# A two-layer encoder trunk in float32 on one core: a tile's work put behind the preparation of the weight group that follows it

## The chip, the cores and the metric

The kernel runs on one core of a Trainium2 chip. The metric is device time in microseconds (us): the median of the runs of one kernel. All multiplications of the large matrices are done in float32r with each operand split in a high part (the value rounded to what TensorE keeps) and a low part (the rest), so that one product is three matmuls: high by high, high by low, low by high.

## What is computed

The input is 256 rows of 2048 columns. Each of the two layers mixes (layer 0: a convolution branch and a gated recurrence; layer 1: two kinds of attention), normalizes, and then runs the feed-forward stage on which this change bears:

```
x = layer_norm(ALPHA * x + mixer(x), ln_mix_g[l], ln_mix_b[l])
h = jnp.square(jax.nn.relu(x @ mlp_w1[l])) @ mlp_w2[l]
x = layer_norm(ALPHA * x + h, ln_mlp_g[l], ln_mlp_b[l])
```

`mlp_w1[l]` is 2048 by 8192 and `mlp_w2[l]` 8192 by 2048, so a layer reads 128 MB of weights there, and those weights are used once.

## The kernel before

**Tiles, units, chunks.** The 8192 hidden columns are cut into 4 blocks b of 2048. A block has four tiles of the first product, w1 (b, 0) to (b, 3), 512 hidden columns each, and four of the second, w2. Each tile is done in two halves. A half is a unit of 4 chunks; a chunk is 256 by 512 weights (512 KB), brought by one DMA of SP's queue into one of four places of `raw`. Two of the w2 tiles of a block (three tiles' worth in the last) are done plainly; tiles j = 0 and 1 (in the last block j = 0 only) are instead done by a seven-product (Strassen-like) scheme, each in four groups q = 0 to 3. A group ("seven", b, j, q) takes 2 chunks of weights and the hidden tile q, and is 7 products of 6 matmuls. `block_order` (L89) writes the order of the units out by hand, `UNITS` (L103) joins it: in a block it is w1 halves and groups of the block before, then w1 (b, 2), (b, 0, 0), w1, (b, 0, 1), both halves of w1 (b, 3), (b, 0, 2), w2 (b, 2) half 0, (b, 0, 3), w2 (b, 2) half 1, and so on.

**Who prepares what.** For each chunk ScalarE copies `raw` to `w_hi` (`split`, L686), VectorE subtracts to get `w_lo` (`split`, L1022), which also lets SP load `raw` anew: `load` (L489) waits for `lo_ready` of the chunk four before. A group needs more. On VectorE `seven_raw` (L1473) waits for both chunks to land and for the products of the previous group (`chunk_used`, as both groups use one buffer), then forms sums of quarters of the weights (L1484, L1486, L1487) and low parts (L1489, L1492). On ScalarE `seven_raw` (L901) copies the high parts (L906, L908). `seven_forms` makes high (L913) and low (L1498) parts of the four sums.

**What a finished tile of w1 asks for.** On ScalarE `hidden_square` (L877: relu from PSUM L883, square L885), `hidden_hi` (L895), and `sums_hi` (L899). On VectorE `sums_added` (L1448: four sums of quarters of the hidden tile, L1456 to L1460, behind the square), `hidden_lo` (L1462: L1034, and L1466 for odd tiles; tile 3's L1034 is in two pieces) and `sums_lo` (L1471), which signals `s_ready`.

**The order around the change.** Both engines take their instructions in the order in which their `mlp` function writes them (L915, L1501). It walks the units; at unit n it does the tile that `finished(n)` (L128) names, the one whose second half ended just before n (groups in between skipped), and prepares what `behind_unit(n)` (L115) names: the groups and the one plain unit that follow n. So during unit n on TensorE the weights behind it are made ready.

**What TensorE waits for.** `seven_products` (L2104) first waits for `s_ready` of hidden tile (b, q), then for the chunks' `lo_ready`, then twice for the forms (`t_lo`), before the 4th and before the 6th product. `out_chunk` (L2067) waits for `h_ready`, `hidden_half` (L2057) for `lo_ready`, both chunk by chunk, and a tile's first matmul for its PSUM bank (`acquire_mlp`, L2047).

Of the kernel before, what the change touches and what calls it, by code (L numbers as in the profile page):

```python
# [102 lines left out]
UNITS = [unit for b in range(FB) for unit in block_order(b)]  # L103
# [11 lines left out]
def behind_unit(n):  # L115

    last = len(UNITS) - SPLIT_BEHIND
    if n < SPLIT_AHEAD:
        return [n + 2] if n == 1 else []
    if n >= last - 1:  # L120
        return [m for m in ((last, last + 1) if n == last - 1 else (n + 2,)) if m < len(UNITS)]
    m = n + 1
    while UNITS[m][0] == "seven":
        m += 1
    return list(range(n + 1, m + 1))


def finished(n):  # L128

    while n and UNITS[n - 1][0] == "seven":  # L130
        n -= 1
    if n and UNITS[n - 1][0] == "w1" and UNITS[n - 1][3] == 1:
        return UNITS[n - 1][1:3]
    return None
# [93 lines left out]
def used_before(s):  # L228
    return BEFORE[s]
# [20 lines left out]
def trunk(nc, x, ev_w_in, ev_conv_w, ev_conv_b, ev_conv_ln_g, ev_conv_ln_b, hgrn_lb_logits, ev_gnorm_g, ev_w_out,  # L250
          od_w_in, fox_b_f, rel_bias, od_w_out, ln_mix_g, ln_mix_b, mlp_w1, mlp_w2, ln_mlp_g, ln_mlp_b, out):
    w_in, w_out = [ev_w_in[0], od_w_in[0]], [ev_w_out[0], od_w_out[0]]
    with ExitStack() as ctx:
# [110 lines left out]
        def form(buf, f, n=1):  # L364

            return buf[:, BESIDE + f * FORM:BESIDE + (f + n) * FORM].rearrange("p (f k n) -> p f k n", f=n, k=CK)
# [12 lines left out]
        seven = [p[:, :].rearrange("p (u n) -> p u n", n=S) for p in pair]  # L379
# [102 lines left out]
        def raw_wait(eng, s):  # L482

            eng.wait_ge(raw_full[s % RING], 16 * (s // RING + 1))
# [187 lines left out]
        def _(act):  # L672
            at = [0]
            n = [0]
# [226 lines left out]
            def seven_raw(layer, m):  # L901

                s = SLOT_MLP[layer] + UNIT_SLOT[m]
                raw_wait(act, s)
                act.wait_ge(chunk_used, used_before(s) + 1)
                act.activation(form(seven_hi, 0)[:, 0], raw[:, s % RING, :, 0:S], ACT.Copy).then_inc(hi_ready, 1)  # L906
                raw_wait(act, s + 1)
                act.activation(low_rows(seven_hi), raw[:, (s + 1) % RING], ACT.Copy).then_inc(hi_ready, 1)  # L908

            def seven_forms(layer, m):  # L910
                for two in range(2):
                    act.wait_ge(t_ready, 2 * seven_no(layer, UNITS[m]) - 1 + two)
                    act.activation(form(seven_hi, 3 + 2 * two, 2), form(forms, 3 + 2 * two, 2), ACT.Copy).then_inc(t_hi, 1)  # L913

            def mlp(layer):  # L915
                base = SLOT_MLP[layer]
                for n, (kind, b, i, half) in enumerate(UNITS):
                    if kind == "seven":
                        if half == NT - 1:
                            act.wait_ge(chunk_used, base + UNIT_SLOT[n + 1])  # L920
                            act.activation(u_sum[:, 0], seven[0][:, 1], ACT.Copy).then_inc(p1_copied, 1)
                        continue
                    done = finished(n)
                    if done and done != (0, 0):
                        hidden_square(layer, *done)
                        hidden_hi(layer, *done)
                    if n == SPLIT_AHEAD:
                        done = (0, 0)
                        hidden_hi(layer, 0, 0)
                    ahead = behind_unit(n)  # L930
                    for m in ahead:
                        if UNITS[m][0] == "seven":
                            seven_raw(layer, m)
                    if done and n != SPLIT_AHEAD - 1:
                        sums_hi(layer, *done)
                    for m in ahead:
                        if UNITS[m][0] == "seven":
                            seven_forms(layer, m)
                            continue
                        for c in range(HALF):  # L940
                            if n == 1 and c == 2:
                                hidden_square(layer, 0, 0)
                            split(base + UNIT_SLOT[m] + c)
                if layer == 0:
                    for c in range(RING):
                        split(base + MLP_SLOTS + c)
                at[0] = base + MLP_SLOTS + RING
# [55 lines left out]
        def _(dve):  # L1003
            at = [0]
            n = [0]
# [442 lines left out]
            def sums_added(layer, b, i):  # L1448

                if b == 0 and i == 0:  # L1450
                    dve.wait_ge(h_back, layer + 1)
                else:
                    dve.wait_ge(h_row, hidden_no(layer, b, i) + 1)
                rows0, rows1, first, second = slice(0, P), slice(P, S), slice(0, CK), slice(CK, 2 * CK)
                h, to = h_turned[i % 2], s_sum[i]
                one = mark(dve.tensor_tensor(to[:, 0], h[:, first, rows1], h[:, second, rows1], ALU.add))  # L1456
                dve.tensor_tensor(to[:, 2], h[:, first, rows0], h[:, first, rows1], ALU.subtract)
                dve.wait_ge(dve_link, one)
                link(dve.tensor_tensor(to[:, 1], to[:, 0], h[:, first, rows0], ALU.subtract))
                dve.tensor_tensor(to[:, 3], h[:, second, rows0], to[:, 1], ALU.subtract).then_inc(s_added, 1)  # L1460

            def hidden_lo(layer, b, i):  # L1462
                dve.wait_ge(h_hi, hidden_no(layer, b, i) + 1)
                if i % 2:

                    dve.tensor_tensor((c_lo7, c_lo15)[i // 2], h_turned[1][:, 3], c_hi[:, 4 * i + 3].bitcast(F32), ALU.subtract)  # L1466
                c_lo_from(h_turned[i % 2], 4 * i, 4).then_inc(h_ready, 1)

            def sums_lo(layer, b, i):
                dve.wait_ge(s_hi_ready, hidden_no(layer, b, i) + 1)  # L1470
                dve.tensor_tensor(s_lo[:, i], s_sum[i], s_hi[:, i].bitcast(F32), ALU.subtract).then_inc(s_ready, 1)  # L1471
# [22 lines left out]
            def seven_forms(layer, m):  # L1494
                for two in range(2):
                    f = 3 + 2 * two
                    dve.wait_ge(t_hi, 2 * seven_no(layer, UNITS[m]) - 1 + two)
                    dve.tensor_tensor(form(seven_lo, f, 2), form(forms, f, 2), form(seven_hi, f, 2).bitcast(F32), ALU.subtract  # L1498
                                      ).then_inc(t_lo, 1)

            def mlp(layer):  # L1501
                base = SLOT_MLP[layer]
                for n, (kind, b, i, half) in enumerate(UNITS[:-1]):
                    if kind == "seven":
                        continue
                    if added(n):
                        add_block(layer, *added(n), 1)
                    done = (0, 0) if n == SPLIT_AHEAD else finished(n)
                    if n == SPLIT_AHEAD - 1:
                        done = None  # L1510
                    if done:
                        sums_added(layer, *done)
                        hidden_lo(layer, *done)
                    ahead = behind_unit(n)
                    for m in ahead:
                        if UNITS[m][0] == "seven":
                            seven_raw(layer, m)
                    if done:
                        sums_lo(layer, *done)
                    for m in ahead:  # L1520
                        if UNITS[m][0] == "seven":
                            seven_forms(layer, m)
                    if n and UNITS[n - 1][0] == "seven" and UNITS[n - 1][3] == NT - 1:
                        add_seven(layer, *UNITS[n - 1][1:3])
                    if kind == "w2" and half == 1:
                        add_block(layer, b, i, 0)
                    for m in ahead:
                        if UNITS[m][0] != "seven":
                            for c in range(HALF):
                                split(base + UNIT_SLOT[m] + c)  # L1530
                at[0] = base + MLP_SLOTS

                def first_rows():
                    add_block(layer, FB - 1, NT - 1, 0)

                second_rows = [lambda: None, lambda: None, lambda: add_block(layer, FB - 1, NT - 1, 1)]
                if layer == 0:
                    upto(SLOT0[1] + RING - 1)
                    layer_norm(2, SLOT0[1], first_rows, second_rows, RT * NT - 1, 0)
                else:  # L1540
                    last_norm(first_rows, second_rows, RT * NT - 1)
# [635 lines left out]
```

## Time and profile before

| what | value |
|---|---|
| runs: median (lowest to highest) | 2192.14 us (2186.53 to 2194.45) |
| the profiled execution's own time | 2188.45 us |
| its span, first to last instruction | 2186.7 us |
| TensorE busy with matmuls | 2166.7 us, 99% of the span |
| VectorE / ScalarE / GpSimd busy | 1678.4 us (77%) / 1166.1 us (53%) / 46.3 us (2%) |
| mean granted TensorE clock | 0.998 of full |
| moved by DMA | 419.29 MB, mean 192 GB/s |
| layer 1's feed-forward stage, 1535 to 2170 us | TensorE busy 635.00 of 635.00 us, clock 1.00 |
| a group on TensorE, start to start of the next unit | 689.63 - 684.87 = 4.76 us |

The span is what the core did between its first and last instruction. "Busy" of TensorE is modelled, as matmuls are pipelined, so whether it truly has no pause is read from the starts in its timeline. A timeline's row has the start, the duration, the engine, the line of the kernel, what is written and read, and in brackets how long the engine stood idle before it and what ended that.

### The profile page before, as it was taken

To read this page: it belongs to the slowest core of one execution; us is meant where nothing else is said; L and a number is where in the kernel's file an instruction comes from. 1 tells how busy PE (TensorE), PEld (TensorE's weight loads), DVE (VectorE), ACT (ScalarE), POOL (GpSimd) and SP (SyncE) were. 2 spreads that over 40 slices of the span, in tenths; PEclk is the share of its full clock that TensorE was granted. 3 is DMA by queue.
4 is the path that set the end of the run, shared out by engine and by line. 5 is a ranking of instruction groups with operands and counts; after the bars stand their busy time and mean duration, and the time that the engine had idled before them with its cause. 6 is when DMAs were issued, how large, how long until landed. Compare 5 with 4: busy or idle time off the path is not lost.

```text
span 2186.7 us, 36813 instructions
## 1 busy us (share of the span) xinstructions
PE 2166.7 (99%) x15395; PEld 2014.2 (92%) x15395; DVE 1678.4 (77%) x2014; ACT 1166.1 (53%) x1300; POOL 46.3 (2%) x77
## 2 busy tenths in 40 slices
PE   9999999999999999999999999999999999999998
PEld 9998888799999999899889999988989999999996
DVE  5999987878788688788675455568787887887886
ACT  5555575455466466466444444444655555555562
POOL 2000010000000000000100000000000000000000
PEclk9999999999999999999999999999999999999999
DMA  7555545556666656666846555565566666566564
GB/s 253 174 164 151 178 154 185 183 189 195 206 199 212 192 189 205 198 201 210 262 138 207 177 172 169 176 201 175 178 192 199 205 193 212 192 196 207 193 220 169
DMA packets 213238, 419.29 MB, mean 192 GB/s; under 512 B 12809, under 2 KB 13377, under 8 KB 212176
## 3 DMA queue, kind: packets, MB, share of 16 engines
q1 hardware_dynamic: 210832, 406.37, 58.4%
q0 software_dynamic: 1952, 10.04, 1.3%
q8 instruction: 121, 1.98, 0.4%
q10 hardware_dynamic: 288, 0.52, 0.1%
q14 instruction: 45, 0.37, 0.1%
HBM read 414.79 MB, written 2.10 MB: 191 GB/s over the span
## 4 chain that ended last, share of the span: by engine, by line
PE 89%; DMA 4%; DVE 4%; ACT 1%; issue 1%; DVEq 0%; POOL 0%; SPq 0%; ACTq 0%
PE gemm L1669 15%; PE gemm L1672 15%; PE gemm L1671 15%; PE gemm L1645 10%; PE gemm L1647 10%; PE gemm L1646 10%; PE pair L2096 4%; PE pair L2098 4%; PE pair L2100 4%; DMA raw<-in_mlp_w 3%; DVE w_lo L1022 1%; PE pair L1828 1%; ACT w_hi L686 1%; DMA raw<-in_od_w_in 1%; PE pair L1786 0%
## 5 line engine op out<-in xcount | busy, mean ns | idle before, releaser
L686 ACT ACTIVATE w_hi<-raw 128x1024 fp32r<-128x1024 f32 x656 | 686.5, 1058 | 662.6 <-PE gemm L1672 235.1
L1022 DVE TENSOR_TENSOR w_lo<-raw,w_hi 128x1024 fp32r<-128x1024 f32 x656 | 787.6, 1224 | 292.9 <-ACT w_hi L686 285.8
L1669 PE MATMUL gemm<-x_hi,w_hi 128*128 128x256 f32 x2912 | 807.3, 277 | 0.0
L1671 PE MATMUL gemm<-x_lo,w_hi 128*128 128x256 f32 x2912 | 805.8, 277 | 0.0
L1672 PE MATMUL gemm<-x_hi,w_lo 128*128 128x256 f32 x2912 | 805.8, 277 | 0.0
L1669 PEld LDWEIGHTS gemm<-x_hi,w_hi 128*128 128x128 f32 x2912 | 548.2, 188 | 1.2 <-issue 0.7
L1671 PEld LDWEIGHTS gemm<-x_lo,w_hi 128*128 128x128 f32 x2912 | 547.3, 188 | 0.6
L1672 PEld LDWEIGHTS gemm<-x_hi,w_lo 128*128 128x128 f32 x2912 | 547.0, 188 | 0.0
L1645 PE MATMUL gemm<-w_hi,c_hi 128*128 128x512 f32 x832 | 325.4, 391 | 1.1 <-issue 1.1
L1646 PE MATMUL gemm<-w_lo,c_hi 128*128 128x512 f32 x832 | 324.0, 389 | 0.0
L1647 PE MATMUL gemm<-w_hi,c_lo 128*128 128x512 f32 x818 | 319.0, 390 | 0.0
L1645 PEld LDWEIGHTS gemm<-w_hi,c_hi 128*128 128x128 f32 x832 | 156.3, 188 | 32.7 <-issue 1.5
L1646 PEld LDWEIGHTS gemm<-w_lo,c_hi 128*128 128x128 f32 x832 | 156.2, 188 | 31.7
L1647 PEld LDWEIGHTS gemm<-w_hi,c_lo 128*128 128x128 f32 x818 | 153.5, 188 | 32.3
L913 ACT ACTIVATE w_hi<-scr 128x1024 fp32r<-128x1024 f32 x112 | 118.4, 1062 | 35.4 <-DVE scr L1487 19.0
L1484 DVE TENSOR_TENSOR scr<-raw 128x1024 f32<-128x1024 f32 x56 | 68.5, 1224 | 83.6 <-issue 57.3
L1498 DVE TENSOR_TENSOR w_lo<-scr,w_hi 128x1024 fp32r<-128x1024 f32 x112 | 131.8, 1219 | 0.0
L1645 PE MATMUL gemm<-w_hi,x_hi 128*128 128x512 f32 x320 | 130.3, 407 | 0.3
L1647 PE MATMUL gemm<-w_hi,x_lo 128*128 128x512 f32 x320 | 125.8, 393 | 0.0
L1646 PE MATMUL gemm<-w_lo,x_hi 128*128 128x512 f32 x320 | 125.4, 392 | 0.0
L2096 PE MATMUL pair<-w_hi,s_hi 128*128 128x256 f32 x448 | 124.5, 278 | 0.0
L2098 PE MATMUL pair<-w_lo,s_hi 128*128 128x256 f32 x448 | 123.7, 276 | 0.0
(240 smaller groups left out, 2509.4 us busy)
## 6 DMA issues: line engine op xcount, KB each, us to landing
raw<-in_mlp_w SPq DMA_DIRECT2D x512, 512.0 KB, 4.7
raw<-in_ev_w_in SPq DMA_DIRECT2D x96, 512.0 KB, 3.7
raw<-in_od_w_in SPq DMA_DIRECT2D x96, 512.0 KB, 3.8
raw<-in_ev_w_out SPq DMA_DIRECT2D x32, 512.0 KB, 4.4
raw<-in_od_w_out SPq DMA_DIRECT2D x32, 512.0 KB, 4.6
lnp<-in_ln_mix_g POOLq DMA_DIRECT2D x2, 1024.0 KB, 6.3
lnp<-in_ln_mlp_g POOLq DMA_DIRECT2D x2, 1024.0 KB, 8.1
lnp<-in_ln_mlp_b POOLq DMA_DIRECT2D x2, 1024.0 KB, 8.0
```

What stands on the lines that cost most here:

```text
L686: act.activation(hi_of_chunk(s), raw[:, s % RING], ACT.Copy).then_inc(hi_ready, 1)
L913: act.activation(form(seven_hi, 3 + 2 * two, 2), form(forms, 3 + 2 * two, 2), ACT.Copy).then_inc(t_hi, 1)
L1022: dve.tensor_tensor(lo_of_chunk(s), raw[:, s % RING], hi_of_chunk(s).bitcast(F32), ALU.subtract).then_inc(lo_ready, 1)
L1498: dve.tensor_tensor(form(seven_lo, f, 2), form(forms, f, 2), form(seven_hi, f, 2).bitcast(F32), ALU.subtract).then_inc(t_lo, 1)
L1645: pe.matmul(acc[:, r, :], hi(k + c)[:, rows], high, start=begin, stop=False)
L1646: pe.matmul(acc[:, r, :], hi(k + c)[:, rows], low, start=False, stop=False)
L1647: return pe.matmul(acc[:, r, :], lo(k + c)[:, rows], high, start=False, stop=end)
L1669: pe.matmul(acc[:, m, :], high, hi(k + c), start=begin and m % 2 == 0, stop=False, skip_group_check=True)
L1671: pe.matmul(acc[:, m, :], high, lo(k + c), start=False, stop=False, skip_group_check=True)
L1672: ins = pe.matmul(acc[:, m, :], low, hi(k + c), start=False, stop=end and m % 2 == 1, skip_group_check=True)
L2096: pe.matmul(seven[bank][:, u, :], hi[c], high[:, c, :], start=begin and c == 0, stop=False, skip_group_check=True)
L2098: pe.matmul(seven[bank][:, u, :], hi[c], low[:, c, :], start=False, stop=False, skip_group_check=True)
```

## The change

Where a tile is done and a group follows at the same n, the group's whole preparation is now written ahead of the tile's work, on both engines. ScalarE before: relu, square, `c_hi`, group's raw, `s_hi`, forms. After: raw, forms, relu, square, `c_hi`, `s_hi`. VectorE before: sums, `c_lo`, group's raw, `s_lo`, forms. After: raw, forms, sums, `c_lo`, `s_lo`. Units with only one of the two keep their order, and so do TensorE, SP and GpSimd.

```diff
--- before.py
+++ after.py
@@ -921,21 +921,21 @@
                             act.activation(u_sum[:, 0], seven[0][:, 1], ACT.Copy).then_inc(p1_copied, 1)
                         continue
                     done = finished(n)
+                    ahead = behind_unit(n)
+                    for m in ahead:
+                        if UNITS[m][0] == "seven":
+                            seven_raw(layer, m)
+                            seven_forms(layer, m)
                     if done and done != (0, 0):
                         hidden_square(layer, *done)
                         hidden_hi(layer, *done)
                     if n == SPLIT_AHEAD:
                         done = (0, 0)
                         hidden_hi(layer, 0, 0)
-                    ahead = behind_unit(n)
-                    for m in ahead:
-                        if UNITS[m][0] == "seven":
-                            seven_raw(layer, m)
                     if done and n != SPLIT_AHEAD - 1:
                         sums_hi(layer, *done)
                     for m in ahead:
                         if UNITS[m][0] == "seven":
-                            seven_forms(layer, m)
                             continue
                         for c in range(HALF):
                             if n == 1 and c == 2:
@@ -1508,18 +1508,15 @@
                     done = (0, 0) if n == SPLIT_AHEAD else finished(n)
                     if n == SPLIT_AHEAD - 1:
                         done = None
-                    if done:
-                        sums_added(layer, *done)
-                        hidden_lo(layer, *done)
                     ahead = behind_unit(n)
                     for m in ahead:
                         if UNITS[m][0] == "seven":
                             seven_raw(layer, m)
+                            seven_forms(layer, m)
                     if done:
+                        sums_added(layer, *done)
+                        hidden_lo(layer, *done)
                         sums_lo(layer, *done)
-                    for m in ahead:
-                        if UNITS[m][0] == "seven":
-                            seven_forms(layer, m)
                     if n and UNITS[n - 1][0] == "seven" and UNITS[n - 1][3] == NT - 1:
                         add_seven(layer, *UNITS[n - 1][1:3])
                     if kind == "w2" and half == 1:
```

## Rows read from the trace of the kernel before

Starts are in us from the first instruction; columns of rows 1 and 9 are busy us and instructions in brackets by engine, then the clock, the DMA's share and GB/s.

**Rows 1.** Busy time by engine, with granted clock, in a feed-forward stretch, layer 0
```profile
core 0: us, PE busy (x) PEld busy (x) DVE busy (x) ACT busy (x) POOL busy (x), PEclk, DMA share, GB/s
455.00:1090.00 635.00, 635.00 (x4761) 601.60 (x4761) 502.34 (x556) 358.39 (x366) 7.72 (x13) 1.00 0.64 203
```

**Rows 2.** List of waits: a row of TensorE's (total, times, longest us)
```profile
PEld pair L2096 <- DVE w_lo L1498: 1.3, 8, 0.2
```

**Rows 3.** VectorE's timeline at a C place (start us, us, ...)
```profile
860.23 0.42 DVE L1456 TENSOR_TENSOR scr<-scr 128x256 f32<-128x256 f32 x1 [0.78 <-ACT scr L885]
...
861.70 0.42 DVE L1466 TENSOR_TENSOR w_lo<-scr,c_hi 128x256 fp32r<-128x256 f32 x1
...
863.24 1.22 DVE L1484 TENSOR_TENSOR scr<-raw 128x1024 f32<-128x1024 f32 x1
...
867.56 1.22 DVE L1471 TENSOR_TENSOR s_lo<-scr,s_hi 128x1024 fp32r<-128x1024 f32 x1
868.70 2.35 DVE L1498 TENSOR_TENSOR w_lo<-scr,w_hi 128x1024 fp32r<-128x1024 f32 x2
```

**Rows 4.** VectorE's timeline, a group with no tile beside it
```profile
847.41 1.23 DVE L1484 TENSOR_TENSOR scr<-raw 128x1024 f32<-128x1024 f32 x1 [1.50 <-DMA raw<-in_mlp_w]
...
851.75 2.36 DVE L1498 TENSOR_TENSOR w_lo<-scr,w_hi 128x1024 fp32r<-128x1024 f32 x2
854.01 1.22 DVE L1022 TENSOR_TENSOR w_lo<-raw,w_hi 128x1024 fp32r<-128x1024 f32 x1
```

**Rows 5.** Page, costliest groups: the square on ScalarE (busy, mean ns)
```profile
L885 ACT ACTIVATE scr<-scr 128x1024 f32<-128x1024 f32 x32 | 34.0, 1063 | 1.0
```

**Rows 6.** TensorE's timeline: a w2 unit's start, then groups (b, 0, 3)
```profile
520.56 0.39 PE L1645 MATMUL gemm<-w_hi,c_hi 128*128 128x512 f32 x1
...
531.47 0.28 PE L2096 MATMUL pair<-w_hi,c_hi 128*128 128x256 f32 x1
...
1038.67 0.28 PE L2096 MATMUL pair<-w_hi,c_hi 128*128 128x256 f32 x1
...
2116.88 0.28 PE L2096 MATMUL pair<-w_hi,c_hi 128*128 128x256 f32 x1
```

**Rows 7.** ScalarE's timeline: the second chunk of the group at the eight C places
```profile
522.34 1.06 ACT L908 ACTIVATE w_hi<-raw 128x1024 fp32r<-128x1024 f32 x1 [0.68 <-DMA raw<-in_mlp_w]
...
691.16 1.04 ACT L908 ACTIVATE w_hi<-raw 128x1024 fp32r<-128x1024 f32 x1
...
862.23 1.06 ACT L908 ACTIVATE w_hi<-raw 128x1024 fp32r<-128x1024 f32 x1 [0.42 <-DMA raw<-in_mlp_w]
...
1029.96 1.06 ACT L908 ACTIVATE w_hi<-raw 128x1024 fp32r<-128x1024 f32 x1 [0.62 <-DMA raw<-in_mlp_w]
...
1600.77 1.06 ACT L908 ACTIVATE w_hi<-raw 128x1024 fp32r<-128x1024 f32 x1 [0.29 <-DMA raw<-in_mlp_w]
...
1769.91 1.06 ACT L908 ACTIVATE w_hi<-raw 128x1024 fp32r<-128x1024 f32 x1 [0.45 <-DMA raw<-in_mlp_w]
...
1939.36 1.06 ACT L908 ACTIVATE w_hi<-raw 128x1024 fp32r<-128x1024 f32 x1 [0.65 <-DMA raw<-in_mlp_w]
...
2110.02 1.06 ACT L908 ACTIVATE w_hi<-raw 128x1024 fp32r<-128x1024 f32 x1 [1.64 <-DMA raw<-in_mlp_w]
```

**Rows 8.** A: VectorE's L1484 of three groups, TensorE's units behind two of them
```profile
778.60 1.22 DVE L1484 TENSOR_TENSOR scr<-raw 128x1024 f32<-128x1024 f32 x1 [0.18 <-issue]
...
947.24 1.23 DVE L1484 TENSOR_TENSOR scr<-raw 128x1024 f32<-128x1024 f32 x1 [0.56 <-issue]
...
958.84 0.28 PE L1669 MATMUL gemm<-x_hi,w_hi 128*128 128x256 f32 x1
...
1688.60 1.23 DVE L1484 TENSOR_TENSOR scr<-raw 128x1024 f32<-128x1024 f32 x1 [1.14 <-issue]
...
1698.91 0.28 PE L1669 MATMUL gemm<-x_hi,w_hi 128*128 128x256 f32 x1
```

**Rows 9.** Busy time and granted clock around TensorE's longest idle time (columns as rows 1)
```profile
219.73:222.15 2.42, 0.00 (x1) 0.00 (x1) 2.42 (x4) 1.06 (x1) 0.00 (x0) 0.95 0.09 12
221.93:225.34 3.41, 3.19 (x15) 3.19 (x16) 3.41 (x8) 1.03 (x1) 0.00 (x0) 0.50 0.48 154
```

## The prediction

> **What bounds the kernel now.** I looked first at TensorE in the stages that the change touches, the two feed-forward stages. Over 635 us of the first, TensorE is busy for all 635.00 us at full clock [rows 1]; the other stage reads the same way in the table above. So nothing there can be won by preparing operands sooner, except where TensorE does wait: the list of waits has one such row, 1.3 us in 8 pieces, for form weights of a group [rows 2]. The question is therefore which operand comes so late in the new order that TensorE runs dry, and the views to read are the timelines of VectorE and ScalarE against the start of the unit on TensorE that wants what they make.
>
> **Where the order changes.** `finished(n)` and a group in `behind_unit(n)` meet at 11 units of each layer, 22 in all, of three sorts. B (8): tile 1 of a block has just ended and the group of weights is the first one, (b, 0, 0). A (6): tile 0 has ended and a group of the previous block, (b-1, 1, 3), follows. C (8): tile 3 has ended and the group is (b, 0, 3). Nothing is added or removed: per place VectorE still has four sums, one or two `c_lo` pieces, `s_lo`, seven instructions of the group and four splits; ScalarE still has its three of the tile, `s_hi` and four of the group. Only the order differs. No transfer is moved, but SP's loads are released by `lo_ready`: the loads four chunks behind a group leave with L1489 and L1492, so earlier, and those four chunks behind the unit that follows leave with its splits, so later where VectorE ends later. GpSimd waits for `chunk_used` alone.
>
> **C, the term that decides.** The old order at one C place: VectorE idles 0.78 us for the square, then sums at 860.23, `c_lo` at 861.70, L1484 at 863.24, `s_lo` at 867.56, forms at 868.70 [rows 3]. `s_lo` ends at 868.78. TensorE starts the group (b, 0, 3) at 869.60, and `seven_products` asks there for `s_ready` of tile 3 before anything else: 0.8 us to spare. In the new order `s_lo` stands last.
>
> How long does the new order take? Call X the start of L1484. Without a tile in between, the group takes from L1484 to the next instruction 854.01 - 847.41 = 6.60 us [rows 4]. Behind it come the sums, 861.70 - 860.23 = 1.47; `c_lo` with its extra piece, 863.24 - 861.70 = 1.54; and `s_lo`, 1.22 [rows 3]. `s_ready` comes at X + 10.83. ScalarE keeps up: its second form activation follows L1487, so it ends about X + 3.8, and relu, square and `c_hi` at about 1.06 us each [rows 5] end by X + 7.0, the square by X + 5.9 before the sums want it at X + 6.60; `s_hi` starts behind the sums and ends at about X + 9.3, before `s_lo` starts at X + 9.61.
>
> And X? L1484 waits for both chunks of the group to have landed and for the previous group's last product, since both groups use one buffer. That product ends when the w2 unit starts; the unit lasts 531.47 - 520.56 = 10.91 us [rows 6]. So had the chunks landed by then, `s_ready` would come at 10.83 and nothing would be lost. The stall is thus nearly the time by which the second chunk lands after that moment. ScalarE's L908 starts with that landing where it shows an idle time for the DMA [rows 7]; in one of the eight it shows none, and its start is an upper bound. TensorE's starts repeat every (1038.67 - 531.47)/3 = 169.07 us in either layer [rows 6]. L908 + 10.83 - start of the group on TensorE:
> layer 0: 533.17 - 531.47 = 1.7; 701.99 - 700.54 = 1.5; 873.06 - 869.60 = 3.5; 1040.79 - 1038.67 = 2.1.
> layer 1: 1611.60 - 1609.67 = 1.9; 1780.74 - 1778.74 = 2.0; 1950.19 - 1947.81 = 2.4; 2120.85 - 2116.88 = 4.0.
> Sum 19.1 us. Everything upstream of these landings (the unit behind tile 3's second half) keeps its order, so I take the landings as they are. Ends for the unknown: 0 if all land in time, 8 x 4.0 = 32 if all are as late as the last. Behind the stall TensorE is fed: the four splits of the next unit then end from X + 12.0 on, 1.14 apart, and that unit begins only when the group's 4.8 us (table above) are over.
>
> **A.** The group itself is ready in time: its last form ends at X + 6.7, in the tightest case 1695.3 [rows 8], and TensorE asks for it five products of seven into the 4.8 us that end at 1698.91. But the tile's work now lies between the group and the splits of the next first-product unit: 6.60 + 1.47 + about 1.2 + 1.14 + one split of 1.22 = X + 11.6. X is not earlier than before, because the landing set it; the sums used to fill that wait for the DMA. TensorE wants the chunk at 1698.91 against 1688.60 + 11.6 = 1700.2: 1.3 us; at 789.77 (958.84 less 169.07) against 778.60 + 11.6 = 790.2: 0.4; at 958.84 against 947.24 + 11.6 = 958.8: nothing [rows 8]. Ends 0 and 6 x 1.3 = 7.8; I take 2, one of the tight kind and the rest near the other two.
>
> **B.** No group ran just before, so X waits only for the landing and for VectorE's last split; the 0.78 us for the square is hidden, and the forms come before `s_lo`. That takes away the wait of [rows 2]: a gain of 1.3 us. The first split behind it is 0.8 us earlier at best, and up to about 1.5 us later where the lag of A delays the landing. Ends: a gain of 1.3 and a loss of 8 x 1.3 = 10; I take the gain, since with neither end the group itself is late.
>
> **The clock.** One row shows what a dry TensorE can cost besides: it stood idle for 2.42 us from 219.73, and the granted clock was 0.50 (the 1.2 GHz level) over 3.41 us from 221.93 [rows 9]; what it ran in that stretch took twice its time, so 1.7 us were lost. Two of the eight stalls are longer than 2.42 us, so I add 2 x 1.7 = 3.4; the ends are 0 and 8 x 1.7 = 13.6. The Trainium skill, "TensorE: Matmul & The Clock Gate", section "HAM oscillation", describes a kernel that waits for data between bursts of matmuls and finds its clock halved at every burst. By that rule the term would be 13.6 and not 3.4. The trace here neither shows nor excludes it for stalls below 2.4 us inside a dense stage.
>
> **Sum.** 19.1 + 2 + 3.4 - 1.3 = 23.2 us on the profiled execution's own 2188.45 us. That execution lies 3.7 us below the median of the runs, 2192.14; on the median the forecast is 2215.3, say 2215 us. About 0.5% (11 us) is what a measurement of this kernel can tell from no change.
>
> **Rivals.**
> 1. Not slower: the chunks land in time. The point is sharp: as soon as the second chunk of a C group has landed when the previous group ends, 10.83 fits into 10.91 and the stall is gone; then the rest is 2 - 1.3, some 2193 us, and 11 us of loss remain only if the mean lateness stays above 1.3 us of the present 2.4. For it: B starts its group up to 3.8 us sooner, so loads leave sooner, and transfers take anything between 4 and 6 us. Against it: two whole units lie between B and C, in which ScalarE waits for TensorE, so a lead is lost there; and all eight rows are late, by 1.5 us at least. Chance 0.07.
> 2. VectorE does not catch up. Where a tile's 3.8 us of work no longer fills a wait for the DMA, VectorE ends later, its splits release the loads later, and the next landing is later again: the ring of four raw chunks becomes the bound at A and B too. Price: A 6 x 1.3 and B 8 x 1.3 instead of 2 and 0, 16 us more: 2231. For it: VectorE was busy for 502 of these 635 us [rows 1], and the chain in the page's list ends through DMA and VectorE. Against it: ScalarE waits for TensorE in every block, and there the lag is made good. Chance 0.15.
> 3. The clock falls at all eight stalls: 10 us more, 2225. Chance 0.12.
> 4. The change does nothing: the order of the program moves but semaphores impose the old one. For it: X is set by landings. Against it: each engine takes its instructions as written, and in the old rows the sums run while L1484 waits. 2192. Chance 0.03.
> The forecast keeps 0.63. The range of 2203 to 2231 takes in C at a little over half without the clock, as well as rivals 2 and 3, and leaves out rivals 1 and 4 and the far tail above. Slower by over 0.5% is 0.87 (forecast, rivals 2 and 3, less the low edge); within 0.5% 0.10; faster by more 0.03.
>
> **What the profile would show.** TensorE below 635 us busy in that window by some 12 us; in the list of waits a new row, TensorE's L2096 on `s_lo` of L1471, 8 times, 1.5 to 4 us each, about 19 us; some two of them followed by a clock of 0.5; L1669 on L1022 at up to six places, 2 us; the row of L2096 on L1498 gone. L1484 starting within 0.1 us of L908 at C, and `s_lo` ending 10.8 us behind it. I am wrong if TensorE stays dense, if L1471 is in no wait of TensorE, or if the stalls sit at A and B.

## The result, and the profile after

The changed kernel takes 2220.93 us (median of 5 runs, 2218.29 to 2228.44) beside 2192.14 for the kernel before: 28.8 us more, a ratio of 1.014 with a 95% interval of 1.0121 to 1.016. That is slower, well clear of the 11 us that the prediction set as what can be told. The profiled execution is one of the longer ones, 2226.47 us with a span of 2224.7; against the span before it is 38.0 us longer. The ratios here and below are not exactly those of two medians, so that a difference in us comes out somewhat larger or smaller by one than by the other. One execution of a_only and one of b_only, at 2706 us and a mean granted clock of 0.75, count in the medians below and not in the ratios.

Busy time in the two feed-forward stretches of the profile after (first row layer 0, second layer 1; columns as in [rows 1]):

```profile
core 0: us, PE busy (x) PEld busy (x) DVE busy (x) ACT busy (x) POOL busy (x), PEclk, DMA share, GB/s
455.00:1090.00 635.00, 624.89 (x4709) 592.32 (x4708) 496.42 (x552) 353.22 (x362) 1.10 (x2) 1.00 0.60 198
1535.00:2170.00 635.00, 623.94 (x4721) 595.32 (x4721) 487.20 (x544) 350.77 (x359) 0.58 (x1) 0.99 0.60 193
```

TensorE was dense [rows 1]; now it lacks 10 to 11 us in each. The list of waits after says for what (total us, times, longest; PEld is TensorE's weight load, PE the matmul):

```profile
PEld pair L2093 <- DVE s_lo L1471: 19.5, 8, 3.7
...
PE pair L2093 <- DVE s_lo L1471: 16.1, 8, 3.3
...
PEld gemm L1666 <- DVE w_lo L1022: 6.7, 8, 1.8
```

L2093 and L1666 are the lines that were L2096 and L1669 before. The row of [rows 2] is gone. The weight load and the matmul of one stall are two rows, not two stalls. Measured from the start of the matmul ahead to the start of the one that waited, less the same step in the kernel before ("from start to start" below), the eight cost 17.4 us: 1.2, 1.8, 3.2, 2.1 in layer 0 and 1.3, 3.1, 1.2, 3.4 in layer 1.

One C place from VectorE's timeline after, to hold against [rows 3]:

```profile
868.28 1.22 DVE L1484 TENSOR_TENSOR scr<-raw 128x1024 f32<-128x1024 f32 x1 [2.69 <-DMA raw<-in_mlp_w]
...
872.61 2.35 DVE L1498 TENSOR_TENSOR w_lo<-scr,w_hi 128x1024 fp32r<-128x1024 f32 x2
874.88 0.42 DVE L1456 TENSOR_TENSOR scr<-scr 128x256 f32<-128x256 f32 x1
...
877.89 1.22 DVE L1471 TENSOR_TENSOR s_lo<-scr,s_hi 128x1024 fp32r<-128x1024 f32 x1
```

and TensorE's timeline at the same place:

```profile
875.70 0.40 PE L1644 MATMUL gemm<-w_hi 128*128 128x512 f32 x1
879.16 0.39 PE L2093 MATMUL pair<-w_hi,c_hi 128*128 128x256 f32 x1 [3.06 <-DVE s_lo L1471]
```

VectorE now stands idle for 2.69 us until the landing, in front of a tile whose work it could have done, and `s_lo` ends at 879.11, 10.83 us behind L1484. TensorE starts 0.05 us later. From L1484 to the start of `s_lo` it is 9.60 or 9.61 us at the seven other C places as well.

Three stretches of half clock lie behind three of these stalls (same columns as above):

```profile
1052.08:1055.50 3.42, 3.42 (x16) 3.42 (x17) 3.42 (x4) 2.06 (x3) 0.00 (x0) 0.50 0.32 96
1803.02:1806.43 3.41, 3.41 (x18) 3.41 (x17) 3.41 (x4) 1.35 (x2) 0.00 (x0) 0.50 0.46 136
2151.18:2158.00 6.82, 5.98 (x28) 5.98 (x29) 5.33 (x5) 2.98 (x4) 0.00 (x0) 0.50 0.45 135
```

That is 13.65 us at 1.2 GHz; compared with the starts before, they cost 1.7, 1.6 and 2.9 us, the pauses themselves not counted. TensorE had been idle, by start-to-start delay, for 2.1, 3.1 and 3.4 us ahead of them. The fall of the clock at 221.93 before [rows 9] did not come in this execution, though the idle time ahead of it did, 2.4 us again.

### The profile page after: what moved, and what is told of

Same layout as the page of the kernel before. It is cut to its first block, busy times and chain, and to the rows that moved or that the text cites. A ratio compares the mean times of both kernels' runs of the same rounds, so it can differ in the third digit from the quotient of the medians.

```text
span 2224.7 us, 36813 instructions
## 1 busy us (share of the span) xinstructions
PE 2183.5 (98%) x15395; PEld 2027.8 (91%) x15395; DVE 1678.5 (75%) x2014; ACT 1164.1 (52%) x1300; POOL 46.7 (2%) x77
## 4 chain that ended last, share of the span: by engine, by line
PE 32%; DVE 9%; DMA 8%; issue 1%; ACT 1%; DVEq 0%; ACTq 0%
DMA raw<-in_mlp_w 8%; PE gemm L1642 5%; PE gemm L1644 5%; PE gemm L1643 5%; PE gemm L1666 4%; PE gemm L1669 4%; PE gemm L1668 4%; DVE w_lo L1022 2%; DVE scr L1484 1%; PE pair L2093 1%; DVE w_lo L1498 1%; PE pair L2097 1%; PE pair L2095 1%; DMA raw<-in_od_w_in 1%; DVE scr L1486 1%
## 5 line engine op out<-in xcount | busy, mean ns | idle before, releaser
L1666 PE MATMUL gemm<-x_hi,w_hi 128*128 128x256 f32 x2912 | 810.2, 278 | 5.1 <-DVE w_lo L1022 5.0
L1669 PE MATMUL gemm<-x_hi,w_lo 128*128 128x256 f32 x2912 | 807.9, 277 | 0.0
L1666 PEld LDWEIGHTS gemm<-x_hi,w_hi 128*128 128x128 f32 x2912 | 547.9, 188 | 8.1 <-DVE w_lo L1022 6.7
L1669 PEld LDWEIGHTS gemm<-x_hi,w_lo 128*128 128x128 f32 x2912 | 547.5, 188 | 0.0
L1484 DVE TENSOR_TENSOR scr<-raw 128x1024 f32<-128x1024 f32 x56 | 68.6, 1225 | 133.2 <-DMA raw<-in_mlp_w 80.3
L1498 DVE TENSOR_TENSOR w_lo<-scr,w_hi 128x1024 fp32r<-128x1024 f32 x112 | 131.8, 1218 | 0.0
L2093 PE MATMUL pair<-w_hi,s_hi 128*128 128x256 f32 x448 | 125.5, 280 | 0.0
```

The costliest lines, as they stand in the source:

```text
L1666: pe.matmul(acc[:, m, :], high, hi(k + c), start=begin and m % 2 == 0, stop=False, skip_group_check=True)
L1669: ins = pe.matmul(acc[:, m, :], low, hi(k + c), start=False, stop=end and m % 2 == 1, skip_group_check=True)
L2093: pe.matmul(seven[bank][:, u, :], hi[c], high[:, c, :], start=begin and c == 0, stop=False, skip_group_check=True)
```

## The experiments

All keep the whole computation. "Group first" is the order of the change. Places are named as in the prediction. The helper used in all of them:

```diff
+ORDERS = {3: 'group first'}      # tile index of a finished tile: its order; any other "tile first"
+def order_of(done):
+    return ORDERS.get(done[1] if done else None, "tile first")
...
+                    order = order_of(done)
+                    if order in ("group first", "raw first"):
+                        for m in groups:
+                            seven_raw(layer, m)
+                    if order == "group first":
+                        for m in groups:
+                            seven_forms(layer, m)
```

with the tile's work behind it, and the rest of the group where it stood before; the same on both engines. My theory: the loss is the late `s_lo` at C, with a little from A, and half clock behind the long pauses. Rival: VectorE and the ring of raw chunks fall behind wherever the order is changed.

**One sort of place at a time**

c_only, `ORDERS = {3: 'group first'}`. Expected:

> New order only at the 8 places where tile 3 has ended (C). If the loss is the late s_lo of the group (b, 0, 3): eight waits of TensorE on L1471, 17 to 20 us together, plus up to 1.7 us for each piece of half clock, so 18 to 26 us slower than before, most of the whole change's 29. If instead VectorE falling behind in general is what costs, C is one of three equal parts: some 10 us.

a_only, `ORDERS = {0: 'group first'}`. Expected:

> New order only at the 6 places where tile 0 has ended (A). Late s_lo cannot matter here, only the first split behind the group: six waits of TensorE on L1022, 5 us together as in the changed kernel, 4 to 8 us slower. If the ring of raw chunks were the bound: 10 us or more, with waits at the B places that follow as well.

b_only, `ORDERS = {1: 'group first'}`. Expected:

> New order only at the 8 places where tile 1 has ended (B). By the forecast's steps a gain: the eight short waits of TensorE on L1498 go, 1.3 to 1.9 us, and nothing else changes, so 0 to 2 us faster, which is hard to tell from no change. If B has its own loss (two waits on L1022 of 0.3 and 1.1 us stood at B places in the changed kernel) without A's lag ahead of it: 1 to 5 us slower.

| kernel | median, us | ratio to before (95%) | TensorE's waits in the feed-forward stages |
|---|---|---|---|
| c_only | 2220.99 | 1.0113 (1.0092 to 1.0134) | `s_lo`, 8 times |
| a_only | 2202.76 | 1.0036 (1.0021 to 1.0051) | first split (`w_lo`), 4 times |
| b_only | 2190.15 | 0.9979 (0.9967 to 0.9990) | none over 0.3 us |

In us, by the ratios, 24.8, 7.9 and -4.6: together 28.1, and the change's 1.014 is 30.7. The parts add, within their intervals of some 2 to 5 us each. The waits of c_only and of a_only, from their lists (in all these kernels the helper shifts the lines: L2122 is the group's first matmul, L1489 `s_lo`, L1695 the w1 matmul, L1040 `split`):

```profile
PEld pair L2122 <- DVE s_lo L1489: 18.8, 8, 3.3
PE pair L2122 <- DVE s_lo L1489: 15.3, 8, 2.8
```

```profile
PEld gemm L1695 <- DVE w_lo L1040: 5.9, 4, 1.9
PE gemm L1695 <- DVE w_lo L1040: 5.1, 4, 1.7
```

C alone has the same eight waits as the whole change, so they need no help from A or B: the rival falls. In c_only's profile the eight cost 16.6 us from start to start, and five stretches of half clock behind them another 8.0, together 24.6 beside the 24.8 by the ratio. A's 7.9 us are at the upper end of what was expected and above its 5.9 us of waits. TensorE's pace can account for the rest: in the feed-forward stages of a_only's profile some 1500 more steps between matmuls than before took 117.8 ns instead of 113.3, 6.8 us (see the last section), though that is one execution. What B gains is not settled by one result (see below).

**A later wait**

all_late: all 22 places group first, and on TensorE

```diff
-                    pe.wait_ge(s_ready, hidden_no(layer, b, q) + 1)
+                    pe.wait_ge(h_ready, hidden_no(layer, b, q) + 1)
...
+                    pe.wait_ge(s_ready, hidden_no(layer, b, q) + 1)
                     product(1, 0, *total(3), *lower(1), first, False).then_inc(chunk_used, 1)
```

> The whole change, but TensorE asks for s_ready only before the third product of a group (the first that reads s_hi and s_lo) and for h_ready at the group's start. If the wait on s_ready binds, each C stall shrinks by the two products ahead of it, 12 x 0.114 = 1.4 us less the c_lo that must be there (X + 9.6 against X + 10.8), so by about 1.2 us: the eight together from 17.4 to about 8 us, and the kernel 10 to 16 us faster than the change (with fewer pieces of half clock), still 12 to 20 us slower than before. If something else of the group is late too (weights, forms), the stalls keep their length.

It took 2213.23 us, 1.0086 (1.0067 to 1.0104), 18.9 us slower than before and so some 12 us faster than the change. What is left at C is a wait on `c_lo`:

```profile
PEld pair L2122 <- DVE c_lo L1052: 5.9, 4, 3.8
PEld gemm L1695 <- DVE w_lo L1040: 5.7, 7, 2.1
...
PE pair L2122 <- DVE c_lo L1052: 4.1, 3, 3.4
```

Against the change, only the place where TensorE asks is different, and the stalls fell from 19.5 to 5.9 us in the same kind of row. So the semaphore of `s_lo` is what binds at C, and not the group's weights. The rest is less than expected (4.8 us from start to start instead of 8), mostly one stall of 3.6 us where the landing was very late. The other costs in its profile's feed-forward stages are 5.3 us at A and B, 2.8 for two stretches of half clock in a row behind that stall, and 7 for the slower pace.

**Half of the move**

c_raw, `ORDERS = {3: 'raw first'}`.

> Half of the move, at the 8 C places only: both engines do the raw part of the group (L1484 to L1492; L906, L908) ahead of the tile, but the forms stay behind s_lo. If s_lo coming last is what costs, it now comes at X + 4.34 + 1.47 + 1.54 + 1.22 = X + 8.6 instead of X + 10.8: only stalls that were above 2.2 us leave a rest, some 1.7, 1.2 and 0.1 us by the forecast's list, together 0 to 4 us, and the kernel is 0 to 5 us slower than before (c_only: 25). If waiting for the landing before the tile is what costs, c_raw keeps most of c_only's loss, 15 us or more.

2195.61 us, 1.0013 (0.9999 to 1.0026), with a single wait of 0.5 us left on `s_lo`: the loss of C is gone, though VectorE waits for the landing in front of the tile just as in c_only. From its timeline, first C place (L1502 was L1484):

```profile
520.76 1.23 DVE L1502 TENSOR_TENSOR scr<-raw 128x1024 f32<-128x1024 f32 x1 [2.38 <-DMA raw<-in_mlp_w]
...
528.09 1.22 DVE L1489 TENSOR_TENSOR s_lo<-scr,s_hi 128x1024 fp32r<-128x1024 f32 x1
```

`s_lo` ends 8.55 us behind the landing instead of 10.83, at 529.31, and TensorE starts the group at 530.91 without having waited. So the wait for the DMA in front of the tile is harmless by itself; it is the sum of landing, whole group and tile that does not fit into the 10.91 us of the w2 unit.

all_raw, `ORDERS = {0: 'raw first', 1: 'raw first', 3: 'raw first'}`.

> Half of the move at all 22 places: raw part of the group first, then the tile with s_lo, forms last. C as in c_raw costs nothing (1.0013), B neither; at A the tile's work still stands between the group's start and the splits, so the first split comes no sooner than in a_only: four to six waits on L1022, 5 us, and the kernel 4 to 10 us slower. If A's loss came from the forms standing ahead of the tile: within 3 us of before.

2199.12 us, 1.0028 (1.0015 to 1.004), 6 us slower. The size fits, the reason that I gave does not: no wait on L1040 is listed, but four on the forms, which now stand behind the tile at A too:

```profile
PEld pair L2122 <- DVE w_lo L1516: 2.8, 4, 1.2
```

The 2.8 us do not fill the 6 us either. Counted from the starts in the trace, in this execution some 2740 of the 7822 steps between matmuls of 256 columns in the feed-forward stages took 117.8 ns and not 113.3 (see the last section), against 87 in the profile before; at 4.4 ns each, 12 us. That could cover it, but this one execution does not show it for the median.

**The change without its C places**

ab_only, `ORDERS = {0: 'group first', 1: 'group first'}`.

> The change with its C places undone: group first at the 6 A and the 8 B places. If the parts add, as a_only (7.9 us slower) and the two results of B (4.6 and 0.2 us faster) stand, 3 to 8 us slower, with no wait on s_lo. If A's lag spoils the B places behind it (in the changed kernel two of eight B places waited, 0.3 and 1.1 us; in b_only none did): 8 to 12 us slower with waits at B.

2195.69 us, 1.0017 (1.0003 to 1.0031): 3.7 us slower, as the parts add up, and no wait on `s_lo`. Undoing C takes away 27 of the change's 30.7 us.

**What B is worth**

b_again is b_only once more. b_forms and b_forms2 are one kernel: at B the tile stays first, and only the forms go ahead of `s_hi` and `s_lo` (VectorE below, ScalarE alike).

```diff
+                    if order == "forms ahead of sums":
+                        for m in groups:
+                            seven_raw(layer, m)
+                            seven_forms(layer, m)
                     if done:
                         sums_lo(layer, *done)
```

> The same kernel as b_only, to see whether its gain stands beside another set of runs of before: 2 to 6 us faster, interval below 1. If the first result was chance: within 1 us.

> At the 8 B places only: the tile first as before, then the group's raw part, then its forms, and s_hi and s_lo behind them. The square's 0.78 us stays unhidden; only the forms come 1.14 us sooner. If b_only's gain is the eight short waits of TensorE on L1498 that go (0.23 us of delay each in the starts), this has the same gain as b_only, 2 to 5 us. If b_only gains by starting the group's chunks earlier, this gains nothing or less than half.

> b_forms again, beside other runs of before: the removal of eight waits of 0.23 us gives 1.9 us, so 1 to 4 us faster; within 1 us either way if the first result was chance.

| kernel | median, us | ratio to before (95%) |
|---|---|---|
| b_only | 2190.15 | 0.9979 (0.9967 to 0.9990) |
| b_again | 2192.3 | 0.9999 (0.9985 to 1.0013) |
| b_forms | 2189.38 | 0.9988 (0.9975 to 1.0001) |
| b_forms2 | 2188.96 | 0.9981 (0.9972 to 0.9990) |

The same program gave 4.6 us less and 0.2 us less, so two results of one program can lie 4.4 us apart. All four lie below 1, on average by 3 us. b_forms, which moves nothing but the forms, gains no less than b_only: this speaks for the eight short waits on L1498, 1.9 us by the starts, being the gain, and against the earlier start of the group. The profile of b_forms, whose pace is that of before (76 long steps for 87), agrees: its feed-forward stages are 2.0 us shorter from start to start, and nearly all of it stands at those eight groups. In the measured times it is not settled, since the gain is no larger than what differs between two results. The b_forms kernel came out 2.6 and 4.2 us faster than before; it cannot be told from b_only.

**A pause without lateness**

pause3: the kernel before, in which TensorE waits at the C groups for a chunk that is ready only later.

```diff
                     pe.wait_ge(s_ready, hidden_no(layer, b, q) + 1)
+                    if j == 0 and q == NT - 1:
+                        pe.wait_ge(lo_ready, base + UNIT_SLOT[n] + S_CHUNKS + 3)
```

> The kernel before, in its old order, with nothing late; but at the 8 C places TensorE waits at the group's start until the third of the next unit's four chunks has its low part (lo_ready), by the rows of before some 3.4 us behind the start. VectorE and ScalarE are not delayed. If what a stall costs is the pause itself and half clock behind it: eight pauses of 2.8 to 4.5 us, some 27 us, plus 1.7 us for each piece of half clock, mostly all eight, so 30 to 42 us slower. If the clock falls only now and then: 27 to 32. If lateness of VectorE were needed for a loss (a pause alone is made good later): under 10.

2227.75 us, 1.0167 (1.0142 to 1.0193), 36.6 us slower. From its list of waits, and two pauses with a stretch 4 us behind the beginning of each:

```profile
PEld pair L2122 <- issue: 29.5, 8, 4.8
```

```profile
1635.80:1638.10 2.30, 0.37 (x2) 0.00 (x0) 2.30 (x3) 1.22 (x2) 0.00 (x0) 1.00 0.38 106
1639.80:1643.20 3.40, 3.40 (x18) 3.40 (x17) 0.00 (x0) 0.00 (x0) 0.00 (x0) 0.50 0.91 301
1809.00:1812.30 3.30, 0.37 (x2) 0.00 (x0) 3.30 (x3) 1.90 (x2) 0.00 (x0) 1.00 0.42 138
1813.80:1817.20 3.40, 3.40 (x18) 3.40 (x18) 0.00 (x0) 0.00 (x0) 0.00 (x0) 0.51 0.92 307
```

The eight pauses were 2.4 to 4.5 us from start to start, 27.6 us together, and behind seven of them (in two cases from within the pause on) the clock fell, for 3.4 us at six and 6.8 us at one, 27.3 us in all. The profiled execution, 2234.71 us, is the longest of its runs and lies 46.3 us above the profiled one of before: 27.6 for the pauses, 12.3 for the half clock by the starts, 4.8 for the slower pace of the last section, and under 2 left. Nothing of a pause is made good later, and no lateness of the other engines is needed for a loss.

## Why the prediction was right

The forecast was 2215 us in 2203 to 2231, slower with 0.87; measured 2220.93, 28.8 us more instead of 23.2. The step that decided, `s_lo` late at C, was right. That the total came so near also has luck in it: the terms of A and of the clock were too small, that of C a little too large, and the pace of TensorE was in no term.

- **TensorE is the bound, so nothing is to be won.** Right: 635.00 busy us became 624.89 and 623.94.
- **C, 19.1 us through `s_ready`.** Right in mechanism and size: eight waits, 19.5 us by the list and 17.4 us from start to start; `s_lo` 10.83 us behind L1484, to the hundredth. The single places moved (3.2 for 3.5, 3.1 for 2.0, 1.2 for 2.4), since the landings did: I took them from before, where ScalarE and VectorE had done other things just ahead. c_only and all_late show that it is this wait.
- **A, 2 us.** The rule X + 11.6 held: after, one L1484 starts at 957.28 and TensorE wanted the split at 968.5 and got it at 969.0. The term was mis-sized: the six places cost 5.1 us from start to start (0.8, 0.7, 0.5, 0.9, 0.5, 1.8), as X came later against TensorE than in the rows of before; and a_only as a whole was 7.9 us slower. I had set the bound at 7.8 and chosen near the loose end from three places.
- **B, a gain of 1.3.** The row of [rows 2] went away, 1.9 us by the starts. Behind A's lag two B places lost 0.3 and 1.1 us instead, which the bounds had held and the sum had not. Alone, B gains about 3 us, within what can just be told.
- **The clock, 3.4 us.** Too low here: three stalls, not two, and one of them with two stretches, 6.2 us. That a dry TensorE can cost clock was right; the rule behind the count, a stall longer than the 2.42 us of [rows 9], was not: the fall came behind one of 2.1 us and not behind one of 3.2. [Rows 9] was also one outcome of two: the same idle time of 2.4 us at the same matmul stands in all 13 profiles of this case, and the clock fell behind it in four (before, a_only, ab_only, b_forms). The Trainium skill's account ("TensorE: Matmul & The Clock Gate", "HAM oscillation") tells of a clock that halves at every wait between bursts; the waits there are of some 3 to 5 us, longer than most of these stalls, so the prediction stretched it when it put it at all eight. So stretched, it nearly fits pause3, where all eight pauses were long and seven had it, and not the change, where the clock stayed up behind the four stalls of 1.2 to 1.8 us and behind one of 3.2.
- **Left over.** Of the 38.0 us between the two profiled executions, 35.7 came about in the feed-forward stages: C has 17.4, A and B 6.4, the clock 6.2, the gain of B -1.9, and a slower pace of TensorE 5.8 (last section). The matmul behind each stall came another 0.1 us late, 1.7 us in all, and nothing of note remains. The other 2.3 us arose outside those stages, where the change has no part. The profile before had nearly no long steps in its feed-forward stages and the profile after had many, so part of the distance between the two profiles, which is larger than the 28.8 us between the medians, is pace.

Rival 2 (the ring becomes the bound) has a grain of truth in A's size, but a_only, b_only and ab_only keep it at a few us. Rival 1 needed landings in time; none of the eight was. Its "anything between 4 and 6" us for a transfer of a chunk was too narrow: in the profile before they took 3.6 to 8.9 us, half of them 4.0 to 5.7.

## What to carry to other kernels

When one engine is dense, as TensorE was here, an earlier operand is worth nothing (beyond the short waits that it ends) and a later one costs its full lateness, so for each reordering ask which item is now last in its slot and when its consumer asks for it: landing plus all work in front, against the length of the unit that covers it. Put what waits for a DMA behind work that is ready, unless all of it still fits; if it must go in front, move only the part that the ring needs (raw before, forms after), and let the consumer ask for each operand just before its first use. To a pause add the clock that may fall behind it (1.6 us a time here, 2.6 to 2.9 where it lasted twice as long), and expect nothing of it to come back.

## What the runs showed of the hardware

- **Pauses and the clock.** In the changed kernel, c_only, all_late and pause3 there were 18 stalls at the C groups of 2.1 us or more from start to start (4, 5, 1 and 8), and behind 16 of them (in six cases from within the stall on) the granted clock was 0.5 for 3.4 us or twice that; the exceptions were 3.2 and 2.9 us long. None of the seven C stalls between 0.6 and 1.8 us in the changed kernel and c_only was followed by it, nor any at an A place (up to 2.1 us, in all_late). The length alone does not decide: the idle time of 2.4 us in layer 0's mixing stage (219.73 to 222.15 in the profile before) had the fall behind it in 4 of 13 profiles, and in b_only the clock was 0.50 for 6.83 us from 291.07 on, where the only idle time of TensorE just ahead was 1.49 us.
- **Two paces at full clock.** In the profile of before nearly all matmuls of 256 columns in the feed-forward stages follow each other every 113.3 ns. In the changed kernel there are stretches at 117.8 ns, with the granted clock at 1.00 all the while: above all from 1545 us on and again from 1894 us on, each until the w2 units around the next C group. Two stretches of 15 us of the profile after, inside w1 units and groups, show it in the count of matmuls (columns as before; a matmul that reaches over an edge is counted too):

```profile
1550.00:1565.00 15.00, 15.00 (x129) 15.00 (x129) 11.02 (x12) 9.14 (x10) 0.00 (x0) 1.00 0.54 158
1700.00:1715.00 15.00, 15.00 (x135) 15.00 (x134) 11.12 (x13) 8.72 (x9) 0.00 (x0) 1.00 0.65 209
```

  The pace changed mostly at a pause or at a change of unit and then held for tens of microseconds; before, the layer 0 projection from 34 to 129 us and the stretch from 136 to 209 us had the longer one. In the feed-forward stages it cost 5.8 us in the profile after, 4.8 in c_only, 6.8 in a_only and 11.8 in all_raw. It does not go by the program alone: b_only and b_again are one kernel, and their profiles have 1219 and 650 long steps there; b_forms and b_forms2 have 76 and 635. What picks it the runs don't show. Differences of 2.5 us between executions of one kernel can come from it; how much of those between two results does is not shown.
